# A two-block forward pass in one kernel: x turned before it is normed, RWKV's inverse on four quarters of the array, a gather from rows side by side, and two turned weights taken in one go

## What is computed

```
first_block:  h = rms_norm(x, norm1_w)                    # x / sqrt(mean(x^2) + 1e-6) * w
              q, k, v, gates.. = split(h @ w_in)
              x = x + concat(dilated_attention(q, k, v), hgrn2(..)) @ w_out      # 8 heads of 64; 4 of 128
              x = x + expert_choice_moe(rms_norm(x, norm2_w), router, 16 experts)  # 32 tokens each
second_block: rwkv7(x @ ..), moba attention, s5 scan      # three branches, gated and merged
              x = layer_norm(a*x + merged @ w_out_2)
              x = layer_norm(a*x + hier_moe(x, 32 experts, top 2))
```

## Time and profile before

| | |
|---|---|
| Median of 3 runs | 1352.02 us (1351.13 to 1353.05) |
| The profiled execution | 1351.26 us, of which its span is 1349.4 us |
| PE busy | 1158.2 us, 86% of the span |
| DVE, ACT, POOL busy | 417.9, 202.6, 123.2 us |
| DMA | 377.31 MB, 280 GB/s over the span |
| Chain that ended last | PE 62%, DMA 29%, DVE 5%, ACT 2% |

### The profile page before, as it was taken

One profiled execution on the slowest core, in us unless ns is written; L12 is line 12 of the kernel. 1 busy time (PEld: TensorE's weight loads), 2 busy tenths in 40 slices (PEclk: granted clock), 3 DMA queues, 4 the chain that ended last, 5 costly groups with the idle time before them and its releaser, 6 DMA issues.

```text
span 1349.4 us, 18767 instructions
## 1 busy us (share of the span) xinstructions
PE 1158.2 (86%) x8146; PEld 632.5 (47%) x8146; DVE 417.9 (31%) x812; ACT 202.6 (15%) x386; POOL 123.2 (9%) x148
## 2 busy tenths in 40 slices
PE   6989897987666666766899999999999699999996
PEld 5745445542222222222455467888776343333332
DVE  4255833011001000100148536632483421111113
ACT  3111422000000000000000013011240131121111
POOL 0010000000003890000025400000000000000000
PEclk9999997998879888888999999999999899999999
DMA  7422719999999999999923453111315619999991
GB/s 288 174 86 103 311 52 427 427 427 426 428 427 427 428 428 426 427 427 427 390 101 125 148 196 125 64 65 64 125 63 210 284 60 420 423 421 422 422 422 68
DMA packets 62396, 377.31 MB, mean 280 GB/s; under 512 B 6128, under 2 KB 7536, under 8 KB 37104
## 3 DMA queue, kind: packets, MB, share of 16 engines
q1 hardware_dynamic: 60736, 369.64, 67.3%
q10 hardware_dynamic: 1584, 6.55, 1.4%
HBM read 375.13 MB, written 1.05 MB: 279 GB/s over the span
## 4 chain that ended last, share of the span: by engine, by line
PE 62%; DMA 29%; DVE 5%; ACT 2%; issue 1%; SPq 0%; DVEq 0%; ACTq 0%
DMA arena<-in_w_expert_up 23%; PE psum L468 11%; PE psum L471 9%; PE psum L2684 7%; DMA arena<-in_expert_w_up 4%; PE psum L1340 4%; PE psum L2708 3%; PE psum L805 3%; PE psum L2719 3%; DMA arena<-in_w_expert_gate 3%; PE psum L2192 2%; PE psum L2295 2%; PE psum L1052 2%; PE psum L1949 2%; PE psum L1370 2%; PE psum L1134 1%
## 5 line engine op out<-in xcount | busy, mean ns | idle before, releaser
L1340 PE MATMUL psum<-arena 128*32 128x256 f32 x2048 | 151.4, 446 | 95.6 <-DMA arena<-in_w_expert_up 57.1
L468 PE MATMUL psum<-arena 128*128 128x512 f32 x352 | 157.6, 598 | 3.2 <-ACT arena L507 1.6
L1340 PEld LDWEIGHTS psum<-arena 128*32 128x32 f32 x2048 | 70.9, 124 | 176.8 <-DMA arena<-in_w_expert_up 73.4
L1370 PE MATMUL psum<-arena 128*32 128x512 f32 x512 | 125.0, 641 | 14.7 <-DMA arena<-in_w_expert_down 9.3
L471 PE MATMUL psum<-arena 128*128 128x256 f32 x544 | 123.0, 382 | 1.0 <-ACT arena L1777 1.0
L2684 PE MATMUL psum<-arena 128*64 128x512 f32 x512 | 116.0, 595 | 1.8 <-DMA arena<-in_expert_w_up 1.8
L471 PEld LDWEIGHTS psum<-arena 128*128 128x128 f32 x544 | 101.5, 189 | 16.9 <-issue 2.2
L468 PEld LDWEIGHTS psum<-arena 128*128 128x128 f32 x352 | 64.8, 190 | 81.4 <-issue 81.1
L1401 DVE TENSOR_TENSOR arena<-arena,psum 128x256 f32<-128x256 f32 x16 | 6.8, 422 | 227.9 <-ACT arena L1384 227.9
L1370 PEld LDWEIGHTS psum<-arena 128*32 128x32 f32 x512 | 31.6, 116 | 95.8 <-issue 71.6
L2684 PEld LDWEIGHTS psum<-arena 128*64 128x64 f32 x512 | 35.8, 137 | 69.0 <-issue 68.5
(11 more groups left out here) (463 smaller groups left out, 1258.3 us busy)
## 6 DMA issues: line engine op xcount, KB each, us to landing
arena<-in_w_expert_gate SPq DMA_DIRECT2D x32, 2048.0 KB, 25.3
arena<-in_w_expert_up SPq DMA_DIRECT2D x32, 2048.0 KB, 26.6
arena<-in_w_expert_down SPq DMA_DIRECT2D x31, 2048.0 KB, 24.7
arena<-in_w_in SPq DMA_DIRECT2D x21, 2048.0 KB, 8.8
arena<-in_expert_w_gate SPq DMA_DIRECT2D x32, 1024.0 KB, 11.5
arena<-in_expert_w_up SPq DMA_DIRECT2D x32, 1024.0 KB, 13.6
arena<-in_expert_w_down SPq DMA_DIRECT2D x32, 1024.0 KB, 10.2
arena<-in_w_out SPq DMA_DIRECT2D x4, 2048.0 KB, 7.9
```

Of the source, the lines that this page charges most:

```text
L468: mm = pe.matmul(o, lhs[:, k, sub * P:(sub + 1) * P], w[:, k, :], start=(k == 0), stop=(k == kt - 1))
L1340: mm = pe.matmul(ps[32 * c:32 * c + 32], xin[:, e, k], w[:, j, 256 * n:256 * n + 256], start=(k == 0), stop=(k == KD - 1))
L1370: mm = pe.matmul(y_ps[at:at + 32, 512 * n:512 * n + 512], hid_T4[:, j, half], w[:, j, 512 * n:512 * n + 512], start=(half == 0 and j == 0) ...
```

## The change

Four edits. (1) PE turns x itself when it has landed. ACT works out the root as before, but takes one root of a constant first. DVE puts the 1/rms of each token on the diagonal of a 128x256 tile; a product of ones with it spreads the numbers over all partitions; DVE copies them to `spread`, and multiplies each turned block by norm1_w and by `spread`. The first job of the projection waits for two blocks of hT at a time. (2) In pair p=2 of the first attention ACT does `turned(2)` and `turned(3)` before `exp(4)`. (3) ACT writes h2 so that the columns of one stationary operand stand side by side. (4) The inverse's 32 matrices stand as 16 even and 16 odd heads (e); for odd ones W, and DT, are kept on the other half of the partitions, so that their products use the two quarters of the array that the even ones leave free, in another bank.

```diff
-        def rms_rows(tag, src, ready, out, scratch):
+        def norm_turned(tag, src, out, weight, scratch, ones, diagonal, spread):
+                act.wait_ge(*count(tag + "_ones", 1))
+                act.activation(sd, ones[:, 0:2], ACT.Sqrt).then_inc(inc(tag + "_root_ready"), 1)
...
             def tensor(pe):
                 pe.wait_ge(*count("first_loaded", 32))
-                pe.wait_ge(*count(*ready))
+                pe.wait_ge(*count("x_loaded", 16))
...
+                pe.wait_ge(*count(tag + "_rows", NT))
+                pe.matmul(bank(7, SEQ), ones, diagonal, start=True, stop=True).then_inc(inc(tag + "_spread"), 1)
...
+                for t in range(NT):
+                    dve.tensor_scalar(diagonal[:, t * P:(t + 1) * P], ident, rs[:, t:t + 1], None, ALU.mult)\
+                       .then_inc(inc(tag + "_rows"), 1)
+                dve.wait_ge(*count(tag + "_spread", 1))
+                step(dve.tensor_copy(spread, bank(7, SEQ)))
...
+                        last = dve.scalar_tensor_tensor(out[:, k], bank(j)[:, (k % 2) * SEQ:(k % 2 + 1) * SEQ], weight[:, k:k + 1],
+                                                        spread, ALU.mult, ALU.mult)
...
-                pe.wait_ge(*count("n1_T", KD // 2))
...
+                            if j == 0 and e == 0 and k % 2 == 0:
+                                pe.wait_ge(*count("n1_T", k // 2 + 1))
...
-                    if norm:
+                    if norm and p != 2:
...
-                    by_four = h2[:, t].rearrange("p (h q j) -> p h j q", h=2, j=4)
-                    mm = pe.matmul(o, by_four[:, k // 4, k % 4], by_tile[:, t, slots], start=(t == 0), stop=(t == NT - 1))
+                    mm = pe.matmul(o, h2[:, t, k * P:(k + 1) * P], by_tile[:, t, slots], start=(t == 0), stop=(t == NT - 1))
...
+                def place(b0, n, e, c2, turned):
+                    return bank(b0 + e)[rows_of((c2 + e * turned) % 2), n * 64:n * 64 + 64]
+
+                def each(b0, lhs, rhs, sem, turned_in, turned_out):
+
+                    for n, e, c2 in blocks:
+                        R = rows_of((c2 + e * turned_in) % 2)
+                        mm = pe.matmul(place(b0, n, e, c2, turned_out), lhs[R, 8 * e + n], rhs[R, 8 * e + n],
+                                       start=True, stop=True)
...
-                    each(0, Cs, D_, "rw_W")
+                    each(0, Cs, D_, "rw_W", False, True)
...
-                        each(2, DT, Ws, "rw_DW")
-                    each(4, Ws, DT, "rw_WD")
+                        if m == 1:
+                            pe.wait_ge(*count("rw_DT_odd", 1))
+                        each(2, DT, Ws, "rw_DW", True, False)
+                        each(4, Ws, DT, "rw_WD", True, True)
+                        continue
+
+                    for n, e, c2 in blocks:
+                        R, o = rows_of((c2 + e) % 2), place(4, n, e, c2, False)
+                        if e:
+                            pe.matmul(o, eye[R], DT[R, 8 + n], start=True, stop=False)
+                        mm = pe.matmul(o, Ws[R, 8 * e + n], DT[R, 8 * e + n], start=not e, stop=True)
```

More of the change, by code:

```diff
@@ L408, in tensor @@
                     mm.then_inc(inc(tag + "_turned"), 1)
+                pe.wait_ge(*count(tag + "_rows", NT))
+                pe.matmul(bank(7, SEQ), ones, diagonal, start=True, stop=True).then_inc(inc(tag + "_spread"), 1)
             def vector(dve):
+                step = vchain(dve)
+                dve.memset(ones, 1.0).then_inc(inc(tag + "_ones"), 1)
                 dve.wait_ge(*count("first_loaded", 32))
+                dve.wait_ge(*count(tag + "_squares", NT))
+                dve.wait_ge(*count(tag + "_root_ready", 1))
+                dve.tensor_scalar(rs, ss, 1.0 / DM, RMS_EPS, ALU.mult, ALU.add).then_inc(inc(tag + "_ms"), 1)
+                dve.wait_ge(*count(tag + "_sd", 1))
+                step(dve.reciprocal(rs, sd))
+                for t in range(NT):
[3 more added lines that the diff above has]
+                step(dve.tensor_copy(spread, bank(7, SEQ)))
                 for j in range(KD // 2):
@@ L414, in vector @@
                     for k in (2 * j, 2 * j + 1):
[L415 to L422, removed]
+                        last = dve.scalar_tensor_tensor(out[:, k], bank(j)[:, (k % 2) * SEQ:(k % 2 + 1) * SEQ], weight[:, k:k + 1],
+                                                        spread, ALU.mult, ALU.mult)
+                    last.then_inc(inc(tag + "_T"), 1)
+            return Stage(tensor=tensor, vector=vector, scalar=scalar)
         the_chain = {}
@@ L499, in two_blocks @@
         hT = cols.take("hT", KD * SEQ).rearrange("p (k s) -> p k s", k=KD)
[L500 removed]
         scratch = cols.take("scratch", DM)
[L502 to L504 removed]
+        norm1 = norm_turned("n1", x_sb, hT, vec["norm1_w"], scratch, cols.take("n1_ones", P), cols.take("n1_diagonal", SEQ),
+                            cols.take("n1_spread", SEQ))
+        cols.release("scratch", "n1_ones", "n1_diagonal", "n1_spread")
         qkv = cols.take("qkv", NT * 3 * HW).rearrange("p (t c) -> p t c", t=NT)
@@ L1816, in rwkv @@
             cols.release("rw_bT", "rw_kT")
-            D_, DT, Ws, Cs = (take(n, 1024).rearrange("p (t g s) -> p t g s", t=NT, g=HEADS) for n in ("D", "DT", "W", "C"))
+            D_, DT, Ws, Cs = (take(n, 1024).rearrange("p (n s) -> p n s", n=16) for n in ("D", "DT", "W", "C"))
             cols.release("rw_D", "rw_W", "rw_C", "rw_L")
@@ L1944, in tensor @@
                 grid = [(t, g, c2) for t in range(NT) for g in range(HEADS) for c2 in range(2)]
-                def each(b0, lhs, rhs, sem):
-                    for t, g, c2 in grid:
-                        R = rows_of(c2)
-                        mm = pe.matmul(bank(b0 + t)[R, g * 64:(g + 1) * 64], lhs[R, t, g], rhs[R, t, g], start=True, stop=True)
+                blocks = [(n, e, c2) for n in range(HEADS) for e in range(2) for c2 in range(2)]
+                def place(b0, n, e, c2, turned):
[5 more added lines that the diff above has]
+                                       start=True, stop=True)
                     mm.then_inc(inc(sem), 1)
@@ L1955, in tensor @@
                         pe.wait_ge(*count("rw_inv", 1))
+                        for n, c2 in [(n, c2) for n in range(HEADS) for c2 in range(2)]:
+                            R = rows_of(c2)
+                            mm = pe.matmul(place(2, n, 1, c2, True), D_[R, 8 + n], eye[R], start=True, stop=True)
+                        mm.then_inc(inc("rw_D_turned"), 1)
                     else:
                         pe.wait_ge(*count("rw_inv_D", m - 1))
-                    each(0, Cs, D_, "rw_W")
+                    each(0, Cs, D_, "rw_W", False, True)
                     if m == 5:
@@ L2838, in _ @@
         def _(pe):
-            turn1.tensor(pe)
+            norm1.tensor(pe)
             hgrn2.tensor(pe)
```

58 lines of the change are left out of this document (27 added, 31 removed).

## The result

The changed kernel takes 1332.03 us (median of four runs, 1331.21 to 1334.15) where the kernel before takes 1351.71 us (four runs, 1351.13 to 1353.05): a ratio of 0.9855, 95% interval 0.9838 to 0.9873. The forecast was 1334.5 us, range 1331.5 to 1341.5. The profiled execution after took 1331.33 us with a span of 1329.5 us, against 1351.26 and 1349.4: 19.9 us less of span.

What follows compares the result with a forecast made beforehand. DMA streaming bounds 200 to 640 us, its start set by the path to 196 us; PE bounds 843 to 945. Gains 4.4 + 6.6 + 0 + 6.5 = 17.5 from 1351.26, plus 0.76 for the median, give 1334.5 us; range 1331.5 to 1341.5.

Steps and rivals of the forecast that it cites:

- Edit 1, forecast 4.4: At the start, the first projection begins at 11.95 instead of 16.36 us, gaining 4.4 us.
- the spread product: At the start, the product of ones with the diagonals, two records of 256 columns, priced at 0.44 us.
- PE still slow at the start: Rival: PE's lower pace lasts into the new product and projection; the start gains 2.3, total 1336.6 us; chance 12%.
- Edit 2, forecast 6.6: In the first attention's pair 2, PE's wait of 4.59 us and slowness behind it (0.89 and 1.17) go: 6.6 us.
- The slow stretch behind the wait: In pair 2, PE's slow products after its wait; if only moved, the gain is 4.6 us.
- Edit 3, forecast 0: At the gather, any gain in the 8.13 us of products lies inside the DMA-bound stretch: 0.
- the room of 3.7 times: At the gather, ScalarE's two rows of 2.18 us can take 3.7 times as long for nothing.
- Edit 4, forecast 6.5: In the inverse, PE time of 26.8 us becomes 20.1; less half the queueing loss, 6.5 us gained.
- The 0.2 us taken off for queueing: In the inverse, half of a possible loss from W'D products using the same quarter twice running; gain 6.7 became 6.5.
- would have given 1342.9: Rival in the inverse: only two quarters work at a time, calls keep 1.92 us; total 1342.9 us; chance 10%.
- The price of four quarters: In the inverse, four quarters at work at once: 30 ns a product, 1.0 us a call instead of 1.92.
- the 2 us added there: At the range's lower end, 2 us beyond all upper-bound gains, for what a gap less on PE may bring.

Runs made afterwards that it cites:

- the repetition: The changed kernel measured and profiled once more with nothing altered: 1332.05 us, 0.9862 of the kernel before.
- edit 1 alone: The kernel before with only the new start (x turned as it comes, root applied when hT is read out): 1346.98 us, 0.996.
- w_start: The changed kernel with 16 unread products of ones by ones ahead of TensorE's first wait: 1334.55 us, 0.9865 of the kernel before.
- w_three: The changed kernel with unread products filling the waits before the RWKV products, in the second routing and, in two places, at the start: 1330.09 us, 0.984.
- edit 3's: The kernel before with only the gather change (ScalarE writes h2 strided, products read side by side): 1351.99 us, 0.9999.
- edit 2 alone: The kernel before with only both turned weights of pair 2 taken ahead of its exponentials: 1346.27 us, 0.9964.
- the grouped order: The changed kernel with the inverse's blocks issued as all e = 0 products, then all e = 1: 1338.0 us, 0.9893 of the kernel before.
- the later measurement: The changed kernel run again unaltered: 1332.05 us, 0.9862 of the kernel before.

## Why the prediction held, step by step

**Edit 1, forecast 4.4, measured 4.06** in the profile, with starts from 11.73 to 12.62 in the executions that have the edit and no filling, and 16.25 to 16.60 without it. Each step came as worked out: transposes behind the vectors' landing, the end of the diagonals before that of the transposes, 1.52 us from product to projection for the 1.56 reckoned. The term that was off is the spread product: 0.90 us and not 0.44, which was two records' share of a long row. It took 0.60 in the repetition and 1.06 in edit 1 alone; in w_start and w_three, whose transposes ran at the full pace, it took 0.70. So a product that stands alone is longer than its share of a row, and the lower pace is at most a part of the rest. Of the rival *PE still slow at the start*, the cost at this product came true, and its second half (up to 1.7 us more in the projection) not. The argument against it, that before the pause of 0.97 was followed by full speed, holds for four of the five executions with that start: edit 3's lost 2.0 us there.

**Edit 2, forecast 6.6, measured 6.73** in the changed kernel and 6.82 alone, at the start of the stream. The slow stretch behind the wait went with the wait; it wasn't moved. The total of edit 2 alone shows 3.4 to 6.4 us by the ratio and 6.1 by the medians. In its profiled execution 0.9 us was given back in the first weights' stream, within that stretch's scatter, and 1.6 in the second; whether the edit has a part in it isn't shown, and the changed kernel, which has the edit, gives nothing back at either.

**Edit 3, forecast 0, measured 0** (0.9988 to 1.0009 alone), for the reason given. The write's 3.87 us were inside the room of 3.7 times, the products' 2 us inside the stream. (That stream fills slices 6 to 19 of the earlier trace rows, up to some 660 us, and not 6 to 18 and 640.)

**Edit 4, forecast 6.5.** From the first call to the chunks: 52.06 to 44.98 us, 7.1 us, with stops for nothing shown of 0.92 and 1.10 in them. The forecast's PE time was 20.1 us; taking the projection's six pieces (22.0), the product of L1979 (1.96) and the stop out of 44.98, 19.9 are left. By the starts of DVE's sums, W and D'W took 0.93 and 1.1 for the 1.0 forecast, W'D 1.84 for 2.0 (8.0 / 4), step 5's 2.1 for 2.1. The 0.2 us taken off for queueing was not lost, and the calls of before took 27.2 us by the same reckoning, not 26.8.

The rule of the Trainium skill ("TensorE: Matmul & The Clock Gate", Part 3: Packing small matmuls), that a weight load overlaps running products only when their row groups differ, would have given 1342.9. The traces do not agree: the array has two row groups for these products, so by that rule two would be at work at most, and a call of 32 would take as long as in the grouped order, 1.7 to 1.85 us; the interleaved ones took 0.93 and, with half of the neighbours on one row group (D'W), 1.1 us.

**Where a reading was weak.** The price of four quarters came partly from 91 ns a product for L1932. More than half of that row ran at half clock; at full clock it is 67 ns (4.26 / 64), well below the 120 that two quarters would need by that reckoning. The conclusion stood, and would have stood more firmly had I read the row's clock with its duration.

**The sum.** 17.5 forecast, 19.9 between the two profiled executions: 4.06 + 6.73 + 7.09 = 17.9 of the edits, 0.9 of the expert stream and 1.6 of the products' clock, both scatter of one execution, less 0.8 in the second routing's gather (16.11 before, 16.88 after) and the rest in parts under 0.3. The medians differ by 19.7 and, in the later measurement, by 18.7 (1350.79 and 1332.05). The changed kernel's second execution has the low clock at the products, 15.67 at the gather, and nearly the same time (1331.57): how much the clock takes at each place varies between executions.

The measured 1332.03 lies only 0.5 us above the lower end of the range, and what kept it inside is the 2 us added there for what a gap less on PE may bring: all gains at their upper bounds alone end at 1333.5. No run singles out such a gain. The edits account for 17.9 us, close to the sum; the 0.8 to 1.8 us beyond them in the medians have no cause shown and are of the size by which single executions scatter. So the four parts came out as worked out, and that the total stayed inside the range was in part luck.

## What to carry to other kernels

The small products here filled the array only in an order whose neighbours go to different quarters; lay out data so that they can, and deal the order so that they do. Read a group's granted clock with its duration before its ns per product becomes a price, and look at a second execution before a difference of 1 or 2 us gets a cause. A short wait in front of a dense run of products costs more than itself; once every dependency there is taken out, products that nobody reads can keep the clock up, if they leave no long gap behind them (stops of 0.6 and 0.5 us between them did no harm in the routing, one of 1.6 us at the start was followed by a fall).

## What the runs showed of the hardware that I had not expected

- Idle stretches of 1.7 us (ahead of the RWKV products) and of 4.1, 2.3, 1.3 and 3.1 us (in the second routing) were followed by a granted clock of 0.50 during the dense work behind them, at a cost of 1.6 and of 1.5 to 2.9 us. Filled, both costs were gone in three of three executions each. The first cost was also missing in one execution of eleven without filling, so an idle stretch makes the fall likely there and not certain.
- At the start, 16 added products, a wait of 1.6 us, and then 1.7 us lost at a granted clock of 0.50; with the gap filled, none. One execution each.
- At the start the clock column says 1.00 while transposes take 0.23 us each; behind 16 products that filled 1.06 to 7 us they take 0.12. In one execution of the kernel before with edit 3 the slow pace lasted until 21 us, at a column of 1.00 all along, and cost 2.0 us.
- Two copies of 128x1024 on ScalarE from SBUF took 2.17 us with side by side output, and 3.87 when each four neighbours go to places 128 elements apart; 16 products whose stationary columns stand four apart took 8.13 us, side by side 5.96 to 6.59 in eight executions.
